# A hybrid decoder layer: weights and pieces carried over a stage border, GELU at another evacuation, another order in the end part

## The reference, cut to what matters

```
D_MODEL, SEQ, DEC_BATCH, DEC_SEQ = 1024, 1024, 8, 8       # 1024 prompt tokens, 8 x 8 sample tokens

def s5_mix(u, h0_re, h0_im, ...):
    ...                                                   # diagonal complex state space, 32 groups of 16
    y = y + d_skip.astype(f32).reshape(S5_GROUPS, S5_GROUP) * uf
    y = jax.nn.gelu(y.reshape(bt, t, S5_W))
    y = y * jax.nn.sigmoid(y @ w_glu.astype(f32))
    return y.astype(u.dtype), hr[:, -1], hi[:, -1]

def trunk_layer(x, s5_re, s5_im, rw_s, rw_shift, pool_buf, start, ...):
    h = rmsnorm(x, g_pre)
    s5_x, s5_z, rw_p, rw_z, pl_x, pl_z, gate_cols = jnp.split(h @ w_in, IN_SPLITS, axis=-1)
    y_s5, n_re, n_im = s5_mix(s5_x, ...)
    y_rw, n_shift, n_s = rwkv_mix(rw_p, ...)              # shift mix, two low-rank products, matrix state per head
    y_pl, n_buf = pool_mix(pl_x, ...)                     # trailing means over 2, 4, 8, 16 rows
    u_s5 = (y_s5 * jax.nn.silu(s5_z)) @ w_up_s5
    u_rw = (y_rw * jax.nn.silu(rw_z)) @ w_up_rwkv
    u_pl = (y_pl * jax.nn.silu(pl_z)) @ w_up_pool
    gates = jax.nn.sigmoid(gate_cols.astype(jnp.float32)).reshape(bt, t, N_BRANCH, D_MODEL)
    merged = gates[:, :, 0] * u_s5 + gates[:, :, 1] * u_rw + gates[:, :, 2] * u_pl
    out = merged.astype(x.dtype) @ w_o
    return x + rmsnorm(out, g_post), n_re, n_im, n_s, n_shift, n_buf
```

## Time and profile before

| | us |
|---|---|
| median of 3 runs | 1465.02 |
| lowest, highest | 1462.95, 1467.26 |
| the profiled execution | 1468.08 |
| its span, first to last instruction | 1466.3 |
| PE busy | 1343.8 |
| DVE, ACT, POOL busy | 726.9, 451.0, 413.8 |

### The profile page before, as it was taken

The page is one execution under the profiler, slowest core; times in us unless marked ns, Lnnn a source line. Parts: engine busy times, 40 slices in busy tenths (PEclk is TensorE's granted clock), DMA queues, the critical chain, the costliest instruction groups (busy, mean ns, idle before and its releaser), DMA issues. The chain is left out here.

```text
span 1466.3 us, 32227 instructions
## 1 busy us (share of the span) xinstructions
PE 1343.8 (92%) x14048; PEld 1226.5 (84%) x14048; DVE 726.9 (50%) x1489; ACT 451.0 (31%) x809; POOL 413.8 (28%) x414
## 2 busy tenths in 40 slices
PE   3798999999489999999999999999999989986997
PEld 3797899999388989899998889899896688886875
DVE  6438527253445646372727365562623539855042
ACT  6122121221324425252525242332424421021131
POOL 6115555553121312122222203131110043245300
PEclk7798999999699999999999999999997999998999
DMA  5431233331521312122232213132216474432342
GB/s 188 82 104 46 68 98 92 110 106 39 130 66 51 97 56 75 58 68 80 69 84 68 77 39 97 51 85 60 68 55 210 113 248 146 139 91 82 122 144 72
DMA packets 165661, 136.98 MB, mean 93 GB/s; under 512 B 33743, under 2 KB 154624, under 8 KB 165392
## 3 DMA queue, kind: packets, MB, share of 16 engines
q1 hardware_dynamic: 159817, 125.03, 29.5%
q10 hardware_dynamic: 5703, 9.89, 2.1%
HBM read 91.36 MB, written 42.34 MB: 91 GB/s over the span
## 5 line engine op out<-in xcount | busy, mean ns | idle before, releaser
L311 PE MATMUL f_ps<-h_hi,fw_hi 128*128 128x384 f32 (+1 forms) x968 | 341.3, 353 | 16.3 <-POOL h_hi L1254 6.1
L313 PE MATMUL f_ps<-h_hi,fw_lo 128*128 128x384 f32 (+1 forms) x968 | 318.1, 329 | 0.0
L1222 POOL TENSOR_TENSOR fw_lo<-fw,fw_hi 128x1024 fp32r<-128x1024 f32 x48 | 115.2, 2399 | 664.1 <-ACT fw_hi L1280 664.1
L312 PE MATMUL f_ps<-h_lo,fw_hi 128*128 128x384 f32 (+1 forms) x864 | 282.4, 327 | 0.0
L311 PEld LDWEIGHTS f_ps<-h_hi,fw_hi 128*128 128x128 f32 x968 | 183.4, 190 | 33.0 <-issue 16.1
L313 PEld LDWEIGHTS f_ps<-h_hi,fw_lo 128*128 128x128 f32 x968 | 183.5, 190 | 0.0
L311 PE MATMUL proj_ps<-h_hi,whi 128*128 128x384 f32 (+1 forms) x504 | 171.2, 340 | 1.1 <-PEq L220 1.1
L312 PEld LDWEIGHTS f_ps<-h_lo,fw_hi 128*128 128x128 f32 x864 | 163.3, 189 | 4.1 <-issue 4.1
L312 PE MATMUL proj_ps<-h_lo,whi 128*128 128x384 f32 (+1 forms) x504 | 166.3, 330 | 0.0
L313 PE MATMUL proj_ps<-h_hi,wlo 128*128 128x384 f32 (+1 forms) x504 | 166.3, 330 | 0.0
L1325 ACT ACTIVATE f_out<-f_ps 128x384 f32<-128x384 f32 (+1 forms) x108 | 50.9, 474 | 240.9 <-PE f_ps L313 240.7
(11 more groups left out here) (426 smaller groups left out, 2635.1 us busy)
## 6 DMA issues: line engine op xcount, KB each, us to landing
fw<-in_w_in_dram SPq DMA_DIRECT2D x36, 512.0 KB, 4.6
projected<-f_out SPq DMA_DIRECT2D x72, 192.0 KB, 1.9
wst<-in_w_in_dram SPq DMA_DIRECT2D x21, 512.0 KB, 5.0
projected<-proj_out SPq DMA_DIRECT2D x17, 544.5 KB, 3.1
f_out<-projected SPq DMA_DIRECT2D x48, 192.0 KB, 2.4
raw<-projected SPq DMA_DIRECT2D x8, 838.5 KB, 7.6
projected<-f_out SPq DMA_DIRECT2D x36, 160.0 KB, 2.1
branch_z<-projected ACTq DMA_DIRECT2D x8, 544.0 KB, 5.0
```

The lines of the kernel that those rows point to most:

```text
L311: pe.matmul(out, whi, xhi, start=first, stop=False)
L312: pe.matmul(out, whi, xlo, start=False, stop=False)
L313: return pe.matmul(out, wlo, xhi, start=False, stop=last)
L1222: pool.tensor_tensor(wlo[:, g % 2], wst[:, g % 2], whi[:, g % 2].bitcast(F32), ALU.subtract).then_inc(fw_lo, 1)
```

## The change

- Two weight blocks of the RWKV stage (`AHEAD`) are loaded and split at the end of the projection stage, which now shares the memory `fw`, `fw_hi`, `fw_lo`. The RWKV stage starts with them in place (`fill_to`, `HEAD`: 12 pieces ahead of `lora`, 8 ahead of `norms`, 4 behind). Tile 7 now has 48 pieces like the others, the sample tile 24.
- The transposes, copies and stores of the new S5 states stand ahead of the last projection unit; on SP they stand ahead of the last block's store.
- GELU is applied where ACT copies y from PSUM; `gelu_part` is gone. `act_y` is now a view of the loaded y, with a step of 136 words between neighbouring tokens. Two GLU units stand ahead of the sample tile's state products, the rest one step earlier each. `low5` waits for all GLU units, since it overwrites y.
- The GLU weights are loaded ahead of y.
- In the end part the tails are turned one block later, their stores stand at gate load 17, and `pool_high`/`pool_low` stand ahead of `up_high`/`lo` of the same block.
- `take_y` waits for all eight stores of a batch.

```diff
+AHEAD = 2
 def load_w(sp, io, e, n):
-    b = FIRST_BLOCKS[n]
+    b = (FIRST_BLOCKS + FILL_BLOCKS[:AHEAD])[n]
...
                 for n in range(len(blocks) + R):
-                    if R <= n < len(blocks):
+                    if R <= n < len(blocks) + AHEAD:
                         sp.wait_ge(lo_done, n - R + 1)
                         load_w(sp, io, e, n)
+                    if n == len(blocks) + R - 1:
+                        sp.wait_ge(fin_sb, 2)
+                        for z, name in enumerate(("re", "im")):
...
                 for u in range(units):
+                    if u == units - 1:
+                        final_states()
                     project(u)
...
                     if k == 0 and b:
-                        act.wait_ge(y_st, 16 * b)
+                        act.wait_ge(y_st, 16 * L * b)
                     act.wait_ge(y_mm, at + 1)
-                    act.activation(ycut[:, gr, :], Q[3][:, 0:n * J5].rearrange("p (g j) -> p g j", g=n), ACT.Copy).then_inc(y_sb, 1)
+                    act.activation(ycut[:, gr, :], Q[3][:, 0:n * J5].rearrange("p (g j) -> p g j", g=n), ACT.Gelu_apprx_tanh).then_inc(y_sb, 1)
...
-BEFORE_SAMPLE = {"turn": 10, "A": 18, "T": 24}
+BEFORE_SAMPLE = {"turn": 8, "A": 16, "T": 24}
+HEAD = {"lora": 12, "ssq": 20, "end": 24}
...
-        act_y, u5, acc = e.early[:, WB:KT], e.early[:, KT + WB:2 * KT], e.early[:, KT:2 * KT]
-        y5 = e.early[:, 0:WB].rearrange("p b (t j) -> p b t j", t=L5)
+        u5, acc = e.early[:, KT + WB:2 * KT], e.early[:, KT:2 * KT]
+        y5 = e.early[:, WB:KT].rearrange("p b (t j) -> p b t j", t=L5)
+        act_y = y5.rearrange("p b t j -> p b j t")
...
+                        sp.dma_start(w5, io["s5_w_glu"][0].rearrange("(k p) m -> p k m", p=P)).then_inc(w5_loaded, 16)
                         sp.dma_start(y5, e.y5_scr).then_inc(y5_loaded, 16)
-                        sp.dma_start(w5, io["s5_w_glu"][0].rearrange("(k p) m -> p k m", p=P)).then_inc(w5_loaded, 16)
...
-                    if q == 12:
+                    if q == 17:
                         sp.wait_ge(taken, 7)
...
                     def low5(c):
                         at, n = CH[c]
-                        dve.wait_ge(f_mm, GLU0 + WB * (c + 1))
-                        dve.wait_ge(u_made, c + 1)
+                        dve.wait_ge(f_mm, GLU0 + WB * 3)
+                        dve.wait_ge(u_made, 3)
...
                     for k in range(WB):
-                        mm = mm_(fps[(GLU0 + q) % 2][:, 0:n], w5[:, k, m * P:(m + 1) * P], act_y[:, k, at:at + n], start=k == 0, stop=k == WB - 1)
+                        mm = mm_(fps[(GLU0 + q) % 2][:, 0:n], w5[:, k, m * P:(m + 1) * P], act_y[:, k, at // L5:(at + n) // L5, :], start=k == 0, stop=k == WB - 1)
...
+                fill_to(HEAD["lora"])
                 lora(Tile(e, 0, True))
+                fill_to(HEAD["ssq"])
                 norms(Tile(e, 0, True))
+                fill_to(HEAD["end"])
...
                     if b == 1:
                         turn_old()
-                        turn_tails(0)
-                    if b in (2, 3):
-                        turn_tails(b - 1)
+                    if b in (2, 3, 4):
+                        turn_tails(b - 2)
```

More of the change, by code:

```diff
@@ L688, in _ @@
                 pool.wait_ge(permd, 3)
+                pool.wait_ge(lo_done, len(blocks) + AHEAD)
             @block.vector
@@ L865, in s5, with final_states @@
                         outputs(b, at - 9)
+                def final_states():
+                    pe.wait_ge(fins, 2)
+                    pe.transpose(Q[0][0:G, 0:P], fin[:, :], e.ident).then_inc(finflip, 1)
+                    for q in range(2):
+                        mm = pe.transpose(Q[1][:, q * P:(q + 1) * P], snew[:, 4 * q:4 * q + 4, :].rearrange("p b g -> p (b g)"), e.ident)
+                    mm.then_inc(finflip, 1)
                 for u in range(units):
+                    if u == units - 1:
+                        final_states()
                     project(u)
@@ L932, in _ @@
                         s5(*divmod(u - FIRST_S5, PER_BATCH))
[L933 removed]
+                    if u % 3 == 2 and u // 3 + R < len(blocks) + AHEAD:
                         split(u // 3 + R)
[L935 to L937 removed]
 FILL_BLOCKS = ([B_S5Z + b for b in range(4)] + [B_RWZ + b for b in range(4)] + [B_PLZ + b for b in range(4)]
@@ L1280, in hi, with evacuate_to @@
                     act.activation(whi[:, g % 2], wst[:, g % 2], ACT.Copy).then_inc(fw_hi, 1)
-                hi(0)
-                hi(1)
+                act.sem_inc(fw_hi, AHEAD)
                 act.sem_inc(f_free, 2)
                 done = [0]
+                def evacuate_to(count):
+                    while done[0] < count // PIECES:
+                        u = done[0]
+                        g, c = divmod(u, 3)
+                        n = CH[c][1]
+                        if g:
+                            act.wait_ge(f_stored[c], 16 * g)
+                        act.wait_ge(f_mm, u + 1)
+                        act.activation(stage[:, c, 0:n], fps[u % 2][:, 0:n], ACT.Sigmoid if FILL_BLOCKS[g] >= B_GATE else ACT.Silu).then_inc(f_free, 1)
+                        if c == 2:
+                            hi(g + 2)
+                        done[0] += 1
                 def gates(t):
@@ L1316, in evacuate @@
                     def evacuate(stage_name):
[L1318 to L1336 removed]
+                        evacuate_to(pieces(i, stage_name))
                     def gate_part(q):
@@ L1372, in body @@
                     if not t.prompt:
-                        evacuate("Z0")
+                        gate_part(0)
+                        gate_part(1)
                         act.wait_ge(ev["zo_mm"], 1)
@@ L1479, in take @@
                         act.activation(rows_s[:, :], Q[3][0:NB * BUF, :], ACT.Copy).then_inc(taken, 1)
+                evacuate_to(HEAD["lora"])
                 gates(Tile(e, 0, True))
+                evacuate_to(HEAD["ssq"])
                 decays(Tile(e, 0, True))
+                evacuate_to(HEAD["end"])
                 for i in range(TILES + 1):
@@ L1517, in _ @@
                             load_pool_gate(g + 2)
+                    if b % 2 and b // 2 < 10:
+                        up_high(N_FILL + 2 + b // 2)
                     if b in (6, 9):
@@ L1939, in _, with fill_to @@
                 issued = [0]
+                def fill_to(count):
+                    while issued[0] < count:
+                        u, part = divmod(issued[0], PIECES)
+                        r, (at, n) = (u // 3) % 2, CH[u % 3]
+                        if part == 0:
+                            if u % 3 == 0:
+                                pe.wait_ge(fw_lo, u // 3 + 1)
+                            pe.wait_ge(f_free, u + 1)
+                        for k in range(2 * part, 2 * part + 2):
+                            mm = split_mm(pe, fps[u % 2][:, 0:n], whi[:, r, k], wlo[:, r, k], e.h_hi[:, k, at:at + n],
+                                          e.h_lo[:, k, at:at + n], k == 0, k == KT - 1)
+                        if part == PIECES - 1:
+                            mm.then_inc(f_mm, 1)
+                        issued[0] += 1
                 def glu(q):
@@ L2023, in fill @@
                     def fill(stage_name):
-                        while issued[0] < pieces(i, stage_name):
-                            u, part = divmod(issued[0], PIECES)
-                            r, (at, n) = (u // 3) % 2, CH[u % 3]
-                            if part == 0:
-                                if u % 3 == 0:
-                                    pe.wait_ge(fw_lo, u // 3 + 1)
-                                pe.wait_ge(f_free, u + 1)
-                            for k in range(2 * part, 2 * part + 2):
-                                mm = split_mm(pe, fps[u % 2][:, 0:n], whi[:, r, k], wlo[:, r, k], e.h_hi[:, k, at:at + n],
-                                              e.h_lo[:, k, at:at + n], k == 0, k == KT - 1)
-                            if part == PIECES - 1:
-                                mm.then_inc(f_mm, 1)
-                            issued[0] += 1
+                        fill_to(pieces(i, stage_name))
                     def quad(bank, rc, oc, col, l, r, h, n=HD, **kw):
@@ L2265, in _ @@
                     body(t)
-                for q in range(2 * WB, 3 * WB):
+                for q in range(2 * WB + 1, 3 * WB):
                     glu(q)
```

156 lines of the change are left out of this document (63 added, 93 removed).

## The result

The changed kernel took 1477.6 us at the median of four runs (1475.3 to 1479.1), the kernel before 1464.4 (1463.0 to 1467.3, four runs). The ratio is 1.0087, 95% interval 1.0066 to 1.0107: slower by 0.9%, where 1462 us, a gain at the edge of what can be told, had been forecast. The profiled execution took 1477.2 us with a span of 1475.5; that of before has 1466.3. So the traces differ by 9.2 us. The medians differ by 13.3, mainly because the profiled execution of before was 3.7 us above the median of its runs.

A forecast was written before the change was run, and what follows sets the result against it. PE, busy 92% of 1466.3 us, was taken to bound the kernel. Gains 16.9 + 4.7 + 1.2 + 7.7 = 30.5 less 27.4 left 3.1 us: 1468.1 to 1465.0 profiled, 1462 at the median, range 1431 to 1471.

The forecast's parts named there:

- part 4: Block 15 in the end part: the new split order removes PE's 6.1 us wait and 1.6 us slow clock, +7.7 us.
- Part 3: From last GLU product to first pooling product: +1.2 us gained, with PE idling 3 us at the first pooling product.
- part 5: GLU products: streaming y with a step of 136 words costs PE 1.75 ns a column, -27.4 us.
- Part 1: Border of projection and RWKV stage: 24 pieces fill PE's 21.7 us wait, +16.9 us.
- Part 2: Sample tile apart from the GLU products' price: waits go and GLU products take the slow-clock stretch, +4.7 us.
- the two optimistic ones: Rivals on the GLU products: PE hides the step, 1434.5 us, chance 0.25; PE pays in part, around 1448, chance 0.12.
- the doubled fetch: Rival on the GLU products: each record fetches its columns twice, 3.5 ns a column, 1522 us, chance 0.08.
- the border gives its gain back: Rival: first tile's chain late or last tile runs dry, 8 to 10 us of Part 1 go, 1471, chance 0.07.

The follow-up runs named there:

- e1: The changed kernel, but PE streams y in the order in which it lies and ScalarE writes the sigmoid back into token order; 1452.8 us.
- e2: The kernel before, with GELU keeping y in (t, j) order, GLU products and inner5 reading it with the step, low5(0) behind the last outer5; 1494.6 us.
- e3: e1 with no pieces at the border ahead of tile 0, and the last tiles' piece counts of before (66 and 30); 1467.8 us.
- e9: e1 with GpSimd's two extra splits behind its last scan product at the end of the projection stage, in place of ahead of it; 1449.7 us.
- e7: e1 with GpSimd's second split of tile 0 held back until the first tile's bC is made; 1450.4 us.

## Why the prediction was wrong, point by point

**What failed.** The largest of three mis-sized terms is part 4. Its "All of it goes: 6.1 + 1.6" priced the moved split at nothing against the 7.7 us, and it had the overlap wrong: GpSimd's split runs beside VectorE, whose 0.22 us instruction becomes 2.51, and the stretch gained 2.1 us. Part 3's wait at the first pooling product was 6.6 us and not 3, and part 5's price 31.3 us and not 27.4. Each of the three misses (5.6, 3.3 and 3.9 us) is by itself larger than the 3.1 us of gain that the forecast had left, and together they put 1477.6 us above its whole range, 1431 to 1471.

**Part 5, the price of a GLU product, had the right mechanism and was 3.9 us too small.** The forecast was 1.75 ns a column from ScalarE's row and 27.4 us; the twelve products take 64.5 us (1.85 ns a column) instead of 33.2, 31.3 more. e1 and e2 show that nothing but the step makes it. PE does not hide it, although it has a factor of two in hand, and doesn't fetch twice. The first product doesn't feel the clock. Its stretch in the changed kernel (length, then busy us of PE, PEld, DVE, ACT, POOL, granted clock, DMA share and GB/s):

```profile
1090.00:1096.00 6.00, 5.46 (x9) 2.58 (x9) 0.42 (x1) 0.00 (x0) 0.00 (x0) 0.57 1.00 361
```

At 0.57 of the clock, so mostly at 1.2 GHz, it took 5.7 us, no more than the next one, which ran at 1.00. Without the step the same product of e1 took 5.5 us at 0.50 and a warm one 2.75. The 2.2 us that the forecast took off for this were thus right. Of the missing 3.9 us, 3.3 are the rate (64.5 us, not 61.2). The prediction had read ScalarE's slope as 1.8 ns and then used 1.75; PE's, between products of 384 and 320 columns, is (5.70 - 4.78) us over 512 columns, 1.80 ns, and ScalarE's is the same ((3004 - 2542) / 256 = 1.80). The Trainium skill, page "Advanced Engine Details and Errata", section "SBUF Cachelines", says that reads that never meet the line of their neighbour again run slower, and how far one may step hangs on the element's size.

**Part 1, the border, came out near its size by luck: misses on both sides offset each other.** 16.9 was forecast; the stretch gained 18.5, and e3 puts the pieces at 15. Missed on the one side: the two extra splits that "cost nothing" were set against PE's work and not against VectorE's; they cost 1.9 us of a wait in the projection stage (e9). The border opened at 380.5, not 379.3: SP issues the y stores ahead of it 1.4 us later than before (369.97 against 368.57), as the whole stage runs later. From the last store's issue the border took 4.9 us, 3.2 to landing and 1.7 until SP issues `raw`, which fits the forecast. GELU at the other evacuation cost one table load and no wait of PE. Then `bC` was forecast for 416.6, with 1.5 us to spare, and came at 421.7: 1.4 from the border, 3.4 from VectorE's three stretched products (e7). Missed on the other side: tile 7 with 48 pieces was put down as "nothing, or 1 us", and it takes away the 2.0 us wait and the 1.6 us of slow clock behind it. (PE's last work at 371.9 was a state transpose; the last projection product had ended at 371.6.)

**Part 2, the sample tile apart from the products, was right in size.** -5.9 us against -4.7 forecast (25.4 less 31.3). The wait of 1.3 us ahead of the first product shrank to 0.5; the forecast's 2.2 us for the y load did not come.

**Part 3 had the right mechanism and too small a size.** -1.2 us was forecast, with PE idle for 3 us at the first pooling product; it was +2.1 and 6.6 us. Two steps failed. "Behind gate load 17, so at about 1202" puts the stores 39.9 us behind the end of the last GLU product; they began 42.1 us behind it (1212.52 - 1170.42), since gate loads 15 to 17 wait for VectorE to free their places: 2.2 us. And "levels 3.2 us" didn't see GpSimd's split beside the first level: 1.2 us more. Together they make up the miss of 3.3.

**Part 4 was half right.** The 6.1 us wait and its slow clock went as forecast. "Done by about 1280" looked at when PE needs a split, and not at what the splits meet: the new order put GpSimd's split of pooling block 2 beside VectorE's last piece of pooling block 3. That took back 2.3 us, with 1.7 more for the slow clock that followed (3.8 us for six products instead of 2.1, at a granted clock of 0.54 behind the 4.2 us wait). The other 1.6 are a result of part 3: behind its wait of 6.6 us the first pooling product ran slow as well (3.7 instead of 2.1, at 0.56). Together with the forecast's own 7.7 this makes the measured 2.1 (7.7 - 2.3 - 1.7 - 1.6 = 2.1).

The likeliest case was thus 1465.0 for a profiled execution against 1477.2: 3.9 of the 12.2 us are in the products' price, 3.3 in the stores, 5.6 in part 4, 1.4 in the projection stage and 0.8 in the output stage, less 2.8 that parts 1 and 2 brought beyond their sums. At the median the miss is 15.6 us (1477.6 against 1462), because the forecast took 3.1 off for a profiled execution of before that lay above its median, and the one of the changed kernel did not. Of the rivals the two optimistic ones are refuted by the products' time, the doubled fetch too. The fourth, "the border gives its gain back", which had the right sign at 1471, is refuted by e3. No rival held the true one: the forecast was a small difference of two large sums, 30.5 and 27.4, and the shortfalls of the first were a wait sized too small and collisions of work that had been weighed only against PE.

## What to carry to other kernels

When a layout change moves a stride from one engine to another, price it on the new engine at the rate at which the old one pays it, and look first for an order in which the busiest engine streams what lies side by side and an idle one takes the step: here that alone turned +0.9% into -0.9%. When work is moved on GpSimd, look at what VectorE does in that moment, not only at what PE does: a 0.2 us instruction on a critical chain can become 2.5 us. A VectorE instruction that takes several times its usual duration and ends just behind one of GpSimd is the sign to look for in the trace of before. When a change makes one thing on the path slower, waits elsewhere hide under it, so taking it back returns less than it cost until these are mended too.

## What the runs showed of the hardware

- PE streaming fp32 columns with a step of 136 words: 1.85 ns a column, 0.89 with runs of 48 neighbours. ScalarE, 1536 elements: 3004 ns with that step and 1484 without. VectorE's `inner5` over 1536 elements took 2.92 us with the step (1.75 before). With the step, a product took as long at a granted clock of 0.57 as at 1.00.
- VectorE instructions that read two SBUF operands stood still while GpSimd's tensor-tensor ran: each of the six of the changed kernel above ended after GpSimd's by no more than the time it takes alone (0.07 to 1.1 us), and those that were moved apart took their 0.22, 0.56, 0.69 and 1.24 us again. The Trainium skill states this, page "SBUF — State Buffer", section "SBUF: two separate sides": the pair of ports that the two share is locked for a whole instruction, and the other one blocks. The traces agree, with GpSimd's instruction the first of the pair each time and VectorE's behind it; the prediction did not reckon with it.
